# Two slabs loaded before a wait, the last recurrences split apart, late slabs four at a step, and keys prepared ahead of state loads

## The chip, the cores and the metric

The kernel runs on one core of a Trainium2 chip. The metric is the device time of one execution in microseconds (us); lower is better. The kernel before takes 1451.17 us, the median of three runs (1448.81 to 1451.53).

## The reference

One inference step of one layer of a hybrid decoder, on 512 prompt tokens and 8 sequences of 4 new tokens (544 columns in all), model width 1024, float32. Cut to what matters:

```python
h = rmsnorm(x) * (1 + sc1) + sh1                       # sh1, sc1, g1, sh2, sc2, g2 = silu(c) @ w_ada + b_ada
q, k, v, g, xr, gr = split(h @ w_in)                   # 1024,1024,2048,2048,1536,1536 wide
o, s_new = retention(rope(q), rope(k), v, s_ret)       # 4 heads, 256 x 512 states, chunks of the prompt
branch_ret = (groupnorm(o) * silu(g)) @ w_br_ret
xconv = causal_conv(xr)                                # width 4
r, i = sigmoid(xconv @ w_a + b_a), sigmoid(xconv @ w_x + b_x)     # blocks of 128
a = exp(-8 * r * softplus(-lru)); h_t = a * h_(t-1) + sqrt(1 - a*a) * (i * xconv)
branch_rnn = (h_t * gelu(gr)) @ w_br_rnn
mixed = (ga * branch_ret + gb * branch_rnn) @ w_out    # ga, gb = sigmoid(h @ w_mgate + b_mgate)
x = x + g1 * rmsnorm(mixed)
x = x + g2 * rmsnorm((silu(fg) * fu) @ w_ffn_out)      # fg, fu = (rmsnorm(x) * (1 + sc2) + sh2) @ w_ffn_in
```

The outputs are x, the new retention states, the last recurrent state and the last three inputs of the convolution.

## The kernel before

All activations stand with channels on the 128 partitions and the 544 columns in the free dimension. A weight matrix comes in **slabs** of 128 output channels: 128 x 1024 numbers (512 KB), for `w_br_rnn` two halves of 128 x 768 (384 KB) per output tile. A slab is loaded by SP into one of two `raw` buffers (`load_to`, L686), ScalarE rounds it to `w_hi` (`split_to`, L1179) and VectorE writes the rest to `w_lo` (L1510); both are rings of three. TensorE multiplies in three passes (hi*hi, hi*lo, lo*hi) with two halves of 272 columns (`three_passes`, L754), so a tile of 8 slab columns is 48 matmuls. A `raw` buffer is free when VectorE has made its `w_lo` (L693), a ring place when TensorE is through with the slab three before. ScalarE and VectorE call `ahead(key)` ahead of a tile, which splits slabs up to two behind it. Tiles alternate between two pairs of PSUM banks: a tile waits (`claim`) until the tile two before it was taken out.

The order of work is written out by hand, once per engine, and each engine runs its own list in order; SP and GpSimd also wait in order for what their DMAs need. Three stretches matter here.

**The start (0 to 75 us).** SP issues the input, 16 slabs of `w_ada` and the slabs of the first two tiles, `xr0` and `gr0` (slabs 0 and 1), and then waits until h is complete (`h_ready`, L709), since `rg_w` (the weights of the recurrent gates, 1.5 MB) and the late slabs lie where the start's buffers lay. Behind that wait it issues `rg_w`, three late slabs (`load_late(ADA_EARLY)`), and all further slabs in order. ScalarE's list behind h: split slab 2 (L1275), evacuate tile `xr0` (L1283 to L1287), split slab 3, evacuate `gr0`.

**The end of the recurrent branch (240 to 375 us).** For n = 0 to 11 the tiles are `xr n`, two gate matmuls, `gr n`, and some tiles `gb m` of the merge gate; at n = 11 four, `gb 4` to `gb 7`, with the gates of block 11 behind `gb 4`. VectorE per n: convolution, split, the recurrence of a block (`decays` and `recur`, L1609 to L1638, thirteen operations with the scan at L1634), splits. At n = 11 blocks 9, 10 and 11 are still to do. After them come eight tiles `bn m` (the projection of the recurrent branch, in two halves of six blocks each; the first tile's halves wait block by block for `y_ready`), and behind each half the modulations of two **late** slabs of `w_ada` (slabs of 512 KB; 32 in all, in a ring of 13, of which 3 places are free from the start and 10 only when the recurrences are done: `recurrences_done`, L712). SP loads late slabs and `bn` slabs in turn in the loop at L720.

**The states (400 to 950 us).** Per head, TensorE works down the tiles and small units of `retention_units` (L158). For each of 8 sequences `b` there is a unit that adds to a state (`sample`, L1040), which needs `k_st`, the keys masked to that sequence, made by GpSimd in three operations (L2060 to L2065), and pairs of sequences have cross products (`cross`, L1020), which need the state loaded. There are four state buffers. GpSimd's list per sequence (L2050): wait for the store of the state two before, load the next into its buffer, prepare the keys, and then store the state before (`store_state`, which waits for VectorE's update).

Of the kernel before, what the change touches and what calls it, by code (L numbers as in the profile page):

```python
# [31 lines left out]
KD = D // P  # L32
SEQ = 512
NB = 8
# [6 lines left out]
H = 4  # L41
# [3 lines left out]
NR = DR // P  # L45
# [27 lines left out]
STATES = 4  # L73
ADA_RING = 13
ADA_EARLY = 3
# [110 lines left out]
GATE_TILES = {1: (0,), 4: (1,), 7: (2,), 10: (3,), NR - 1: (4, 5, 6, 7)}  # L186
# [17 lines left out]
def recurrences_at(n):  # L204

    if n == NR - 1:
        return (n - 2, n - 1)
    return (n - 1,) if n == NR else (n - 2,) if n >= 2 else ()
# [156 lines left out]
def hybrid_layer_kernel(nc, w, out):  # L365
    pl = make_plan()
# [5 lines left out]
    with ExitStack() as top:  # L372
        def sem(name):
            return top.enter_context(nc.semaphore(name))
# [129 lines left out]
        s_stored = [sem(f"s_stored{i}") for i in range(STATES)]  # L504
# [97 lines left out]
        def wait_freed(eng, key):  # L602
            eng.wait_ge(*freed(key))
# [31 lines left out]
        def late_slab(n):  # L635

            i = n % ADA_RING
            return ada_late[:, i, :] if i < ADA_EARLY else ada_more[:, i - ADA_EARLY, :]
# [30 lines left out]
        @block.sync  # L669
        def _(sp):  # L670
            nxt = [0]
            late = [0]

            def load_late(n):

                while late[0] < n:
                    j = late[0]
                    if j == ADA_EARLY:
                        recurrences_done()
                    if j >= ADA_RING:  # L680
                        sp.wait_ge(late_used, j - ADA_RING + 1)
                    sp.dma_start(late_slab(j), w["w_ada"][FIRST_BLOCKS + j // KD, j % KD])\
                        .then_inc(late_in[j % ADA_RING], 16)
                    late[0] += 1

            def load_to(s):  # L686

                while nxt[0] <= s and nxt[0] < len(pl.slabs):
                    i = nxt[0]
                    key, cols = pl.slabs[i]  # L690
                    place, loaded, _, last = raw_slab(i)
                    if last is not None:
                        sp.wait_ge(lo_ready, last + 1)  # L693
                    sp.dma_start(place[:, 0:cols], slab_source(w, key)).then_inc(loaded, 16)
                    nxt[0] += 1

            def load_x(i):
                sp.dma_start(x_in[:, 2 * i:2 * i + 2, :], w["x"][:, 2 * i:2 * i + 2, :]).then_inc(x_loaded[i], 16)

            sp.dma_start(con[:], w["con"]).then_inc(con_in, 16)  # L700
            load_x(0)
            sp.dma_start(vec[:], w["vec"]).then_inc(vec_in, 16)
            for i in range(1, 4):
                load_x(i)
            for n in range(FIRST_BLOCKS * KD):
                if n == KD:
                    load_to(pl.slab[("gr", 0, "w", 0)])
                sp.dma_start(ada_raw[:, n, :], w["w_ada"][n // KD, n % KD]).then_inc(ada_in[n], 16)
            sp.wait_ge(h_ready, KD)  # L709
            sp.wait_ge(c4_ready, 1)  # L710
            sp.dma_start(rg_w[:], w["w_rg"]).then_inc(rg_in, 16)
            def recurrences_done():  # L712

                sp.wait_ge(last_saved, NR)
                sp.wait_ge(tails_saved, NR)
                sp.wait_ge(y_ready, NR)

            load_late(ADA_EARLY)
            load_to(pl.slab[("bn", 1, "w", 0)])
            for m in range(KD):  # L720
                for part in range(2):
                    load_late(min(4 * m + 2 * part + ADA_RING, 4 * KD))
                    load_to(pl.slab[("bn", m, "w", part)] + 2)
            sp.dma_start(out["rnn"], rnn_out[:]).then_inc(stored, 16)
            load_to(pl.slab[("v", 0, 1, "w", 0)])
            rnn_memory_free(sp)
            sp.dma_start(cosin[:], w["cosin"]).then_inc(cosin_in, 16)
            for h in range(H):
                load_to(pl.slab[("k", h, 0, "w", 0)])
                if h:  # L730
                    wait_freed(sp, ("sc", h - 1, JT - 1))
                sp.dma_start(dec[:], w["dec"][h]).then_inc(dec_in, 16)
            load_to(pl.slab[("wo", KD - 2 * EARLY, "w", 0)])

            sp.wait_ge(mix_ready, KD)
            states_stored(sp)
            sp.dma_start(xr_[:], w["x"]).then_inc(xres_in, 16)
            load_to(len(pl.slabs) - 1)
            for half in range(2):
                for k in range(KD):  # L740
                    sp.wait_ge(y_done, KD * half + k + 1)
                    sp.dma_start(out["y"][:, k, cols_of(half)], xr_[:, k, cols_of(half)]).then_inc(stored, 16)
            sp.wait_ge(stored, 16 * (1 + 2 * KD))
# [760 lines left out]
        def _(dve):  # L1504
# [16 lines left out]
            def ahead(key, part=0):  # L1521
                split_to(pl.slab[(*key, "w", part)] + AHEAD)
# [86 lines left out]
            def decays(n):  # L1609


                dve.wait_ge(u_ready, n + 1)
                dve.wait_ge(e_ready, n + 1)
                u, e, root = (t[:, n % 2, :] for t in (uu, ee, su))
                do(V.tensor_scalar(e, e, 1.0, None, ALU.add))
                dve.wait_ge(su_ready, n + 1)
                do(V.scalar_tensor_tensor(u, u, 1.0, e, ALU.add, ALU.mult))
                do(V.scalar_tensor_tensor(e, u, -4.0, e, ALU.add, ALU.mult))
                do(V.tensor_scalar(u, e, -0.5, -1.0, ALU.mult, ALU.add))
# [24 lines left out]
            for n in range(NR):  # L1644
                ahead(("xr", n))
                conv(n)
                ahead(("gr", n))
                for i in recurrences_at(n):
                    decays(i)
                    recur(i)  # L1650
                for m in GATE_TILES.get(n, ()):
                    ahead(("gb", m))
                    if n == NR - 1 and m == GATE_TILES[n][0]:
                        for i in recurrences_at(NR):
                            decays(i)
                            recur(i)
            for m in range(KD):
                split_to(pl.slab[("bn", m, "w", 1)] + AHEAD)
                wait_took(dve, ("gb", m))
# [307 lines left out]
        def _(pool):  # L1967
# [54 lines left out]
            def load_state(u):  # L2022
                h, b = divmod(u, NB)
                pool.dma_start(state[:, u % STATES, :, :], w["state"][b, h].rearrange("(d p) e -> p d e", p=P))\  # L2024
                    .then_inc(s_loaded[u % STATES], 16)
# [11 lines left out]
            for h in range(H):  # L2037
                for e in range(ET):
                    wait_took(pool, ("v", h, e))
                    if h and e == 0:  # L2040
                        wait_full(pool, ("tvs", h - 1))
                    do(G.tensor_copy(v3[:, e, :].rearrange("p (r c) -> p r c", r=3),
                                     vf[:, e % 2, SEQ:T].unsqueeze(1).to_broadcast([P, 3, NS])), v3_ready, wait=False)
                pool.wait_ge(k_ready, h + 1)
                if h:
                    wait_full(pool, ("tks", h - 1))
                do(G.tensor_copy(k3[:].rearrange("p d (r c) -> p d r c", r=3),
                                 k_r[:, :, SEQ:T].unsqueeze(2).to_broadcast([P, 2, 3, NS])), k3_ready, wait=False)
                wait_freed(pool, ("tks", h))
                for b in range(NB):  # L2050
                    u = h * NB + b
                    if STATES <= u + 2 < H * NB:
                        last = u + 2 - STATES
                        pool.wait_ge(s_stored[last % STATES], 16 * (last // STATES + 1))
                        load_state(u + 2)
                    if u >= 2:
                        hh, bb_ = divmod(u - 2, NB)
                        wait_full(pool, ("sn", hh, bb_, 1))

                    do(G.tensor_scalar(k_msk[:, :], k_raw[:, :], ccol("kmask", h * NB + b, 1, 3 * NS), 1.0, ALU.mult,  # L2060
                                       ALU.mult))
                    do(G.tensor_copy(k_st[:, u % 2, :], k_msk[:, :]))
                    lo = slice(2 * NS, 3 * NS)
                    do(G.tensor_tensor(k_st[lo, u % 2, :], k_msk[lo, :], k_st[lo, u % 2, :].bitcast(F32),
                                       ALU.subtract), kst_ready)  # L2065
                    if u:
                        store_state(u - 1)
            store_state(H * NB - 1)
# [108 lines left out]
```

## Time and profile before

| | |
|---|---|
| median of three runs | 1451.17 us |
| profiled execution, its own time | 1449.33 us |
| its span (first to last instruction) | 1447.5 us |
| TensorE matmul busy | 1377.7 us, 95% |
| VectorE busy | 717.9 us, 50% |
| ScalarE busy | 484.3 us, 33% |
| GpSimd busy | 181.3 us, 13% |
| granted TensorE clock, mean | 0.979 |
| DMA | 172.70 MB, mean 119 GB/s |
| slabs `raw` to landing, median | 3.4 to 3.8 us |

The profile is of one execution. Its page gives for each engine the busy share in 40 slices of the span (36 us each): TensorE reads nine tenths or more in nearly all, with lower slices at the start, at about 265, 485 and 1010 us and at the end. The same slices show the granted clock of TensorE in tenths. A wait is put down to the instruction whose semaphore came last; where an engine waits for several, the others can be nearly as late.

### The profile page before, as it was taken

What the parts mean: (1) busy time and instruction counts of PE and PEld (TensorE: products, weight loads), DVE (VectorE), ACT (ScalarE), POOL (GpSimd) and SP (SyncE); (2) the same over time, 40 slices, a digit from 0 to 9 for tenths busy, and PEclk for the clock granted to TensorE, in tenths of its full rate; (3) what the DMA queues carried; (4) which work ended last, traced back from release to release, by engine and by line L of the source; (5) the groups of instructions that cost most, each with busy time, mean ns of one, the idle gap of its engine ahead of it and who ended that gap; (6) DMA issues with size and microseconds to landing.
All of it is one profiled execution on the core that took longest, in us unless ns stands there. A gap on an engine that the chain in (4) does not pass through costs nothing.

```text
span 1447.5 us, 23984 instructions
## 1 busy us (share of the span) xinstructions
PE 1377.7 (95%) x10324; PEld 1281.7 (89%) x10324; DVE 717.9 (50%) x998; ACT 484.3 (33%) x683; POOL 181.3 (13%) x284
## 2 busy tenths in 40 slices
PE   6699999899999899999999999999799999999995
PEld 3599999788997798799889879999799999999995
DVE  4349888522242475267437624966743333332225
ACT  4277778312231231232224123336422222212221
POOL 1013222000113212212320322000000000000000
PEclk8899999999999999999999999999899999999998
DMA  8422222475424434434442443243022222222321
GB/s 340 149 70 73 74 88 74 171 283 180 159 81 147 154 103 132 163 97 141 148 166 67 138 159 133 88 162 120 0 73 88 88 88 88 88 83 81 88 87 62
DMA packets 49930, 172.70 MB, mean 119 GB/s; under 512 B 5537, under 2 KB 7713, under 8 KB 49569
## 3 DMA queue, kind: packets, MB, share of 16 engines
q1 hardware_dynamic: 39456, 135.51, 28.1%
q0 software_dynamic: 9216, 33.56, 6.6%
q10 hardware_dynamic: 1152, 2.10, 0.4%
q8 instruction: 82, 1.34, 0.4%
q14 instruction: 24, 0.19, 0.0%
HBM read 149.82 MB, written 21.32 MB: 118 GB/s over the span
## 4 chain that ended last, share of the span: by engine, by line
PE 82%; DVE 9%; ACT 3%; DMA 3%; issue 2%; POOL 0%; SPq 0%; DVEq 0%; ACTq 0%; POOLq 0%
PE ps L760 66%; PE ps L769 3%; PE ps L1005 2%; PE ps L1016 2%; PE ps L808 1%; PE ps L988 1%; PE ps L1048 1%; PE ps L1034 1%; DMA raw<-in_w_brnn 1%; PE ps L891 1%; DMA raw<-in_w_out 1%; DVE w_lo L1517 1%; DMA raw<-in_w_rnn 1%; DVE x_res L1872 1%; DVE rsn L1867 1%
## 5 line engine op out<-in xcount | busy, mean ns | idle before, releaser
L760 PE MATMUL ps<-h_hi,w_hi 128*128 128x272 f32 x2096 | 444.1, 293 | 22.8 <-ACT xs L1287 9.5
L760 PE MATMUL ps<-h_hi,w_lo 128*128 128x272 f32 x2096 | 436.3, 290 | 0.0
L760 PE MATMUL ps<-h_lo,w_hi 128*128 128x272 f32 x2096 | 435.3, 289 | 0.0
L1517 DVE TENSOR_TENSOR w_lo<-raw,w_hi 128x1024 fp32r<-128x1024 f32 (+2 forms) x190 | 226.5, 1195 | 335.3 <-ACT w_hi L1189 332.9
L760 PEld LDWEIGHTS ps<-h_hi,w_hi 128*128 128x128 f32 x2096 | 333.9, 190 | 36.6 <-issue 18.0
L760 PEld LDWEIGHTS ps<-h_lo,w_hi 128*128 128x128 f32 x2096 | 332.4, 190 | 0.0
L760 PEld LDWEIGHTS ps<-h_hi,w_lo 128*128 128x128 f32 x2096 | 330.2, 190 | 0.0
L1189 ACT ACTIVATE w_hi<-raw 128x1024 fp32r<-128x1024 f32 (+2 forms) x190 | 195.6, 1030 | 355.9 <-PE ps L760 241.5
L1791 DVE SCALAR_TENSOR_TENSOR state<-state,ps 128x512 f32<-128x512 f32 x64 | 41.1, 684 | 111.1 <-PE ps L1048 110.9
L760 PE MATMUL ps<-a_hi,w_hi 128*128 128x272 f32 x308 | 63.8, 288 | 2.1 <-DVE a_lo L1526 2.1
L760 PE MATMUL ps<-a_hi,w_lo 128*128 128x272 f32 x308 | 63.8, 288 | 0.0
L760 PE MATMUL ps<-a_lo,w_hi 128*128 128x272 f32 x308 | 63.5, 288 | 0.0
L760 PE MATMUL ps<-r_hi,w_hi 128*128 128x272 f32 x256 | 53.6, 290 | 0.0
L760 PE MATMUL ps<-r_hi,w_lo 128*128 128x272 f32 x256 | 52.9, 288 | 0.0
L760 PE MATMUL ps<-r_lo,w_hi 128*128 128x272 f32 x256 | 52.8, 288 | 0.0
L760 PEld LDWEIGHTS ps<-a_hi,w_hi 128*128 128x128 f32 x308 | 48.4, 188 | 2.3 <-DVE a_lo L1526 2.3
L760 PEld LDWEIGHTS ps<-a_lo,w_hi 128*128 128x128 f32 x308 | 48.4, 189 | 0.0
L2024 POOL DMA_DIRECT2D state<-in_state x32 | 23.4, 730 | 199.1 <-PE ps L816 104.5
L760 PEld LDWEIGHTS ps<-a_hi,w_lo 128*128 128x128 f32 x308 | 48.1, 189 | 0.0
L760 PEld LDWEIGHTS ps<-r_hi,w_hi 128*128 128x128 f32 x256 | 40.3, 188 | 5.2 <-DVE w_lo L1517 2.5
L1944 DVE TENSOR_TENSOR a_tmp<-a_tmp,ps 128x544 f32<-128x544 f32 x19 | 13.7, 721 | 60.9 <-PE ps L760 60.9
L1197 ACT ACTIVATE a_tmp<-ps 128x544 f32<-128x544 f32 x19 | 11.9, 626 | 95.2 <-PE ps L760 95.2
(238 smaller groups left out, 1848.8 us busy)
## 6 DMA issues: line engine op xcount, KB each, us to landing
raw<-in_w_head SPq DMA_DIRECT2D x48, 512.0 KB, 3.8
raw<-in_w_fin SPq DMA_DIRECT2D x38, 512.0 KB, 3.4
state<-in_state POOLq DMA_DIRECT2D x32, 512.0 KB, 4.1
out_rs<-state POOLq DMA_DIRECT2D x32, 512.0 KB, 3.9
raw<-in_w_rnn SPq DMA_DIRECT2D x24, 512.0 KB, 3.5
ada_more<-in_w_ada SPq DMA_DIRECT2D x23, 512.0 KB, 6.2
ada_raw<-in_w_ada SPq DMA_DIRECT2D x16, 512.0 KB, 14.6
raw<-in_w_bret SPq DMA_DIRECT2D x16, 512.0 KB, 3.5
```

The lines of the kernel that those rows point to most:

```text
L760: mm = nc.tensor.matmul(dst[:, half, :], a, b[:, half * HALF:(half + 1) * HALF], start=first and j == 0, stop=last and j == 2)
L769: mm = nc.tensor.matmul(dst, a, b[:, cols_of(half)], start=first and j == 0, stop=last and j == 2)
L808: mm = nc.tensor.matmul(ps[g * ROWS:(g + 1) * ROWS, bank, 0:ADA_COLS], c_rows[:, k, :], slab[:, g * ADA_COLS:(g + 1) * ADA_COLS], start=k ...
L891: mm = nc.tensor.matmul(dst[:, half, 0:HALF], rg_w[:, n, g, :], xc[:, n % 2, half * HALF:(half + 1) * HALF], start=True, stop=True)
L988: mm = nc.tensor.matmul(dst[:, 0:SEQ - j * P], k_r[:, d, j * P:(j + 1) * P], q_r[:, d, j * P:SEQ], start=d == 0, stop=d == 1)
L1005: mm = nc.tensor.matmul(dst[:, j * P:SEQ], v_tok[:, j, o * P:(o + 1) * P], scores(j), start=j == 0, stop=j == JT - 1, skip_group_check=True)
L1016: mm = nc.tensor.matmul(dst[:, :], k_tok[:, j, d * P:(d + 1) * P], v_tok[:, j, :], start=j == 0, stop=j == JT - 1)
L1034: nc.tensor.matmul(ps[g * NS:(g + 1) * NS, 7, :], q_st[:, d, NS * b:NS * (b + 1)], state[:, u % STATES, d, :], start=pair == 0, stop=pair ...
L1189: A(hi[:, 0:cols], src[:, 0:cols], ACT.Copy).then_inc(hi_ready, 1)
L1517: V.tensor_tensor(lo[:, 0:cols], raw_slab(i)[0][:, 0:cols], hi[:, 0:cols].bitcast(F32), ALU.subtract).then_inc(lo_ready, 1)
L1791: do(V.scalar_tensor_tensor(state[:, u % STATES, d, :], state[:, u % STATES, d, :], gamma(h) ** TS, ps[:, pl.bank[key][0], :], ALU.mult, A ...
L2024: pool.dma_start(state[:, u % STATES, :, :], w["state"][b, h].rearrange("(d p) e -> p d e", p=P))\
```

## The change

It has four parts, in three places.

1. `load_to(gr 1)`, which issues slabs 2 and 3, is put ahead of SP's wait for `h_ready`.
2. At n = 11 VectorE's list was: recurrences 9 and 10, splits for `gb 4`, recurrence 11, splits for `gb 5`, `gb 6`, `gb 7`. It becomes: recurrence 9, splits up to two behind `gb 4`; recurrence 10, splits up to two behind `gb 6`; recurrence 11, splits up to two behind `gb 7`.
3. In the loop of the `bn` tiles SP issues the `bn` slab first and then late slabs, at most to number 3 + 4 * (i + 1) in step i = 2m + part, where the ring's limit of 13 + 2i is not lower. Before, the late slabs came first, up to the ring's limit.
4. GpSimd prepares the keys of a sequence ahead of the wait for a store and the load of the state two further on.

```diff
--- before.py
+++ after.py
@@ -706,6 +706,7 @@
                 if n == KD:
                     load_to(pl.slab[("gr", 0, "w", 0)])
                 sp.dma_start(ada_raw[:, n, :], w["w_ada"][n // KD, n % KD]).then_inc(ada_in[n], 16)
+            load_to(pl.slab[("gr", 1, "w", 0)])
             sp.wait_ge(h_ready, KD)
             sp.wait_ge(c4_ready, 1)
             sp.dma_start(rg_w[:], w["w_rg"]).then_inc(rg_in, 16)
@@ -719,8 +720,9 @@
             load_to(pl.slab[("bn", 1, "w", 0)])
             for m in range(KD):
                 for part in range(2):
-                    load_late(min(4 * m + 2 * part + ADA_RING, 4 * KD))
                     load_to(pl.slab[("bn", m, "w", part)] + 2)
+                    i = 2 * m + part
+                    load_late(min(2 * i + ADA_RING, ADA_EARLY + 4 * (i + 1), 4 * KD))
             sp.dma_start(out["rnn"], rnn_out[:]).then_inc(stored, 16)
             load_to(pl.slab[("v", 0, 1, "w", 0)])
             rnn_memory_free(sp)
@@ -1645,15 +1647,18 @@
                 ahead(("xr", n))
                 conv(n)
                 ahead(("gr", n))
-                for i in recurrences_at(n):
-                    decays(i)
-                    recur(i)
-                for m in GATE_TILES.get(n, ()):
-                    ahead(("gb", m))
-                    if n == NR - 1 and m == GATE_TILES[n][0]:
-                        for i in recurrences_at(NR):
-                            decays(i)
-                            recur(i)
+                if n < NR - 1:
+                    for i in recurrences_at(n):
+                        decays(i)
+                        recur(i)
+                    for m in GATE_TILES.get(n, ()):
+                        ahead(("gb", m))
+                else:
+                    ends = GATE_TILES[n]
+                    for i, until in zip(recurrences_at(n) + recurrences_at(NR), (ends[0], ends[2], ends[3])):
+                        decays(i)
+                        recur(i)
+                        ahead(("gb", until))
             for m in range(KD):
                 split_to(pl.slab[("bn", m, "w", 1)] + AHEAD)
                 wait_took(dve, ("gb", m))
@@ -2049,10 +2054,6 @@
                 wait_freed(pool, ("tks", h))
                 for b in range(NB):
                     u = h * NB + b
-                    if STATES <= u + 2 < H * NB:
-                        last = u + 2 - STATES
-                        pool.wait_ge(s_stored[last % STATES], 16 * (last // STATES + 1))
-                        load_state(u + 2)
                     if u >= 2:
                         hh, bb_ = divmod(u - 2, NB)
                         wait_full(pool, ("sn", hh, bb_, 1))
@@ -2063,6 +2064,10 @@
                     lo = slice(2 * NS, 3 * NS)
                     do(G.tensor_tensor(k_st[lo, u % 2, :], k_msk[lo, :], k_st[lo, u % 2, :].bitcast(F32),
                                        ALU.subtract), kst_ready)
+                    if STATES <= u + 2 < H * NB:
+                        last = u + 2 - STATES
+                        pool.wait_ge(s_stored[last % STATES], 16 * (last // STATES + 1))
+                        load_state(u + 2)
                     if u:
                         store_state(u - 1)
             store_state(H * NB - 1)
```

## Rows read from the trace of the kernel before

**Rows 1.** Waits of TensorE by what they waited for: us in total, times, longest.

```profile
PE ps L760 <- ACT xs L1287: 9.5, 1, 9.5
...
PE ps L760 <- DVE w_lo L1517: 8.5, 4, 5.9
...
PE ps L1048 <- POOL k_st L2064: 4.8, 1, 4.8
```

**Rows 2.** The chain that ended last in order of time: start, us, what.

```profile
52.53 9.54 DMA raw<-in_w_rnn
...
64.68 7.84 PE ps L760 x48
...
309.75 4.73 PE ps L760 x36
...
438.19 6.02 PE ps L760 x48
...
485.73 7.11 PE ps L760 x48
```

**Rows 3.** Windows of 5 us: busy us (instructions) of each engine, clock, DMA, GB/s.

```profile
35.00:40.00 5.00, 5.00 (x48) 3.62 (x48) 0.09 (x1) 0.00 (x0) 0.00 (x0) 1.00 0.00 0
...
60.00:65.00 5.00, 0.32 (x1) 0.35 (x2) 1.65 (x2) 2.85 (x6) 0.33 (x1) 0.50 0.48 196
...
285.00:290.00 5.00, 5.00 (x48) 4.66 (x50) 0.00 (x0) 0.00 (x0) 0.00 (x0) 1.00 1.03 410
```

**Rows 4.** Timeline of 28 to 110 us: start, us, engine, line, operation, idle before.

```profile
33.86 1.23 DVE L1517 TENSOR_TENSOR w_lo<-raw,w_hi 128x1024 fp32r<-128x1024 f32 x1
...
50.60 0.33 SPq L711 DMA_DIRECT2D rg_w<-in_w_rg  x1
...
54.81 0.41 PE L760 MATMUL ps<-h_hi,w_lo 128*128 128x272 f32 x2
...
62.15 1.06 ACT L1189 ACTIVATE w_hi<-raw 128x1024 fp32r<-128x1024 f32 x1 [12.40 <-DMA raw<-in_w_rnn]
```

**Rows 5.** Timeline of VectorE, 242 to 312 us.

```profile
252.97 0.73 DVE L1526 TENSOR_TENSOR y_lo<-bb,y_hi 128x544 fp32r<-128x544 f32 x1
...
253.73 0.45 DVE L1615 TENSOR_SCALAR ee<-ee 128x544 f32<-128x544 f32 x1
...
260.84 1.74 DVE L1526 TENSOR_TENSOR y_lo<-bb,y_hi 128x544 fp32r<-128x544 f32 x1
...
262.61 1.23 DVE L1517 TENSOR_TENSOR w_lo<-raw,w_hi 128x1024 fp32r<-128x1024 f32 x1
```

**Rows 6.** Timeline of TensorE, 242 to 306 us.

```profile
263.98 0.79 PE L760 MATMUL ps<-h_hi,w_hi 128*128 128x272 f32 x2 [5.92 <-DVE w_lo L1517]
...
279.08 0.42 PE L760 MATMUL ps<-y_hi,w_hi 128*128 128x272 f32 x2
...
298.28 0.52 PE L760 MATMUL ps<-y_hi,w_hi 128*128 128x272 f32 x2 [2.11 <-DVE w_lo L1517]
```

**Rows 7.** Timeline of ScalarE, 242 to 312 us.

```profile
246.45 1.05 ACT L1189 ACTIVATE w_hi<-raw 128x1024 fp32r<-128x1024 f32 x1
...
257.77 1.04 ACT L1189 ACTIVATE w_hi<-raw 128x1024 fp32r<-128x1024 f32 x1
```

**Rows 8.** Timeline of GpSimd, 242 to 312 us.

```profile
260.46 1.52 POOL L1995 TENSOR_TENSOR ii<-ii,xc 128x544 f32<-128x544 f32 x1
```

**Rows 9.** Timeline of SP's queue, 242 to 312 us.

```profile
274.17 6.03 SPq L682 DMA_DIRECT2D ada_more<-in_w_ada  x10
...
285.22 0.43 SPq L694 DMA_DIRECT2D raw<-in_w_brnn  x1
```

**Rows 10.** Timeline of TensorE, 476 to 494 us.

```profile
484.51 1.22 PE L1048 MATMUL ps<-v_st,k_st 96*128 96x512 f32 x2 [4.75 <-POOL k_st L2064]
```

**Rows 11.** Timeline of GpSimd, 395 to 560 us.

```profile
478.15 0.78 POOL L2031 DMA_DIRECT2D out_rs<-state  x1 [0.32 <-POOL k_st L2064]
...
482.43 0.77 POOL L2060 TENSOR_SCALAR k_msk<-k_raw,con 96x256 f32<-96x256 f32 x1
```

## The prediction

> **What bounds the kernel now.** The page first: TensorE is busy 95% of the span and heads the chain that ended last, so what can be won is what it waits for. The view of waits says what that is: one wait of 9.5 us on ScalarE's evacuation, four of 8.5 us in all on VectorE's weight splits, one of 4.8 us on GpSimd's masked keys [rows 1]. The three code regions of the diff lie at these three places. The timeline around each then shows why the wait is there, and the chain what a tile costs at either clock: 48 matmuls take 6.02 us, and 7.84 and 7.11 us behind two of these waits [rows 2] (the windows show the granted clock at 0.50 of full speed in 60 to 65 us, which is 1.2 GHz [rows 3]). So each wait costs more than its length.
>
> **Part A, two slabs before the wait for h.** Slab 2 (the second input tile, xr1) and slab 3 (gr1) are issued only at 52.53 us, behind the recurrent weights (1.5 MB) and three late slabs (0.5 MB each), and the first lands 9.54 us later [rows 2, 4]. ScalarE stands at its split until 62.15, and only then evacuates tile 0, for whose bank TensorE waits: its last matmul begins at 54.81, the next tile at 64.68 [rows 2, 4]. `load_to(gr1)` itself waits for the VectorE splits of slabs 0 and 1; the second begins at 33.86 and ends at 35.1 [rows 4]. So both loads are issued by 35.2 us, and the queue is empty in 35 to 40 us (0 GB/s) [rows 3]; they land about 4 us later, long before h is complete at 50.6. SP waited for h anyway, so nothing is queued behind the new wait. Then ScalarE splits slab 2 (1.06), VectorE follows (1.23): about 53.1, earlier than TensorE's end at 55.22; ScalarE evacuates tile 0 by about 53.7. What was next on the queue: the recurrent weights, issued at 50.60, are first in a backlog that was all through by 62.07 with two slabs more in it [rows 2, 4], and are wanted after xr1, at about 61.2 (1.5 MB is 3.8 us at the 410 GB/s of [rows 3]). Slab 4 (gb0) will be issued at 53.1 and land at 61 to 62; it is wanted at 55.2 + 6.0 + 1.8 + 6.0 = 69. ScalarE is held by it for some 2 us after xr1's end and has gr1's 6 us to make this up. Gain: 9.46 of wait and 7.84 - 6.02 = 1.82 of slow clock, 11.3 us. Bounds: 0, if ScalarE found another load late, and 11.3. I take 11.3, for every wait on the way has a row with room.
>
> **Part B, the last recurrences and the late slabs.** Before, VectorE runs two recurrences between two splits: recurrence 10 begins at 253.73, and the split that tile gb6 needs comes at 262.61 [rows 5]. Tile gb5 ends at 263.98 - 5.92 = 258.06, gb6 starts at 263.98, bn0 at 279.08 [rows 6]: 21.02 us for two tiles that take 12.04, so 8.98 lost. After the change the split stands at 253.73 (its ScalarE half is done: 246.45 [rows 7]), ends at 254.96, and gb6 starts at 258.06 without a wait, to 264.1. Recurrence 10 takes 262.61 - 253.73 = 8.88 us, to 263.8, and the split of gb7 behind it (ScalarE half 257.77 [rows 7]) ends at 265.0: a new wait of about 1.0 us. Of the 8.88 one microsecond is a collision: the same subtraction takes 0.73 us once and 1.74 where GpSimd multiplies beside it [rows 5, 8]. The product in question waits for the same scan and moves with it, so I keep the collision; without it the wait is 0.
> The Trainium skill, SBUF — State Buffer, section "SBUF: two separate sides", calls this an exclusive lock: GpSimd and a VectorE operation with two SBUF inputs take turns for a whole instruction. The trace agrees with 1.74 against 0.73 us, and by that rule the collision stays; were it chance, part B would give 1.0 us more.
> Recurrence 11 then begins after the splits of gb7 and bn0's first half (0.96), at 266.0 instead of 263.75, and ends by 273.9 (7.9 us without a collision), with bn0's second split at 274.8. TensorE: gb7 265.1 to 271.1, bn0's first half 4.73 us and the two modulations 1.00 [rows 2], so it wants the second half at 276.8. That covers it by 2 us; it holds because the first half needs recurrences 0 to 5 only.
> The queue: before, ten late slabs from 274.17 and two more stand ahead of bn slab 3, issued at 285.22, and TensorE waits 2.11 us for it at 298.28 [rows 6, 9], the queue being full at 410 GB/s [rows 3]. After, the order on SP is four late, bn slab 3, four late, bn slab 4, four late, bn slab 5, from 273.9 on. At 0.41 MB per us (late 0.52, bn 0.39 MB): slab 3 is through at 280, slab 4 at 286, slab 5 at 292; 2.3 us more for both splits. They are wanted at 288.3, 294.0 and 299.7 (steps of 5.73 us). Room 5 us. Late slabs are taken two at a step and come four at a step: number 3 is wanted at 281.5 and is there by 276. From the fourth step both orders load to the same number and SP waits for the same use, with the bn load now ahead. So 2.11 goes. Part B: 8.98 - 1.0 + 2.11 = 10.1 us. Bounds: 4 (the 2.5 us that a slow clock took from the tile at 263.98, 8.5 instead of 6.0, come back, slab 3's 2.11 stay, and another step waits 1.5) and 11.1.
>
> **Part C, keys ahead of loads.** TensorE stands 4.75 us before 484.51 for the keys of sample 7 [rows 10]. On GpSimd the store of state 5 (478.15, 0.78) comes first, then a wait for the store of state 5 to land and a load (to 482.34), then three operations, from 482.43 to TensorE's start at 484.51, 2.08 us [rows 10, 11]. After: the store no later than 478.15, the keys at once, from 479.0 to 481.1 (478.15 + 0.78 + 2.08 and 0.1 between). TensorE is free at 484.51 - 4.75 = 479.76: a wait of 1.35 is left. With the tile after it at full speed (7.11 - 6.02 = 1.09 [rows 2]) the gain is 4.75 - 1.35 + 1.09 = 4.5 us. The moved loads are late by those three operations at most, 2 us, and in every step the store they wait for takes as long or longer. The view of waits has no row in which TensorE waits for a state's load. The other 31 preparations stand behind nothing that TensorE waits for: 0. Bounds: 2.4 (the collision above on one more operation, +1, and the slow clock kept) and 5.8.
>
> **Sum.** 11.3 + 10.1 + 4.5 = 25.9. The profiled execution took 1449.33 us (span 1447.5), so 1423.4. It lies 1.8 us under the median of the three runs, 1451.17, from which it would be 1425.3; I say 1424. Nothing behind the three places is late next: the page's slices of TensorE are nines between them, VectorE and ScalarE are below that, and both shift with it.
>
> **Rivals.**
> 1. The small new waits (1.0 and 1.35 us) keep a slow stretch behind them: 2.5 + 1.1 us back, 1427.5. For it: a wait of 4.75 us was enough [rows 2, 10]. Against: the 2.11 us at 298.28 was followed by pairs at full speed. Chance 0.10.
> 2. Part A moves the wait: ScalarE takes slab 4's split before it evacuates xr1, so with a late slab 4 (backlog in front of it) TensorE stands before gb0. For a full return slab 4 would have to land 7 us later than worked out: 1435. Chance 0.06.
> 3. Part B's VectorE chain slips: recurrence 11 ends after 276.8, with more collisions, and every bn step waits about a microsecond for its slab: 1430. Against: 2 us of cover. Chance 0.08.
> 4. Slower: the late slabs. SP waits for a bn split before it issues the next four late slabs; if a late slab came after TensorE wanted it, each of the last 13 steps would hold a whole landing, 13 x 3.5 = 45 us, and the time would be 1468. It decides where late slab 2i lands after step i begins. Against: at the second step the lead is 5 us, and it grows by two slabs a step. Chance 0.02.
> The forecast itself 0.74.
>
> **Numbers.** Range 1419 to 1431: below, the waits of 1.0 and 1.35 vanish and the run-to-run spread of 2 us; above, rivals 1 and 3, with rival 2 left out. About 0.2% (3 us) is what can be told from no change. Faster 0.95, same 0.02, slower 0.03.
>
> **What would show it.** Right: xr1's tile starts within 0.5 us of the tile before it, the granted clock is 1.00 in the windows there; gb6 follows gb5 at once; TensorE's waits on w_lo are below 2 us in all; the wait on k_st is 1 to 2 us. Wrong: ScalarE waiting for in_w_gb while TensorE stands, a wait on late slabs at the modulations, a wait on a y tile in bn0, or clock windows under 1.00 behind the small waits.

## The result and the profile after

The kernel after takes 1430.2 us, the median of four runs (1426.68 to 1431.54), against 1451.35 us (1448.81 to 1451.81): a ratio of 0.9854 (95% interval 0.9832 to 0.9876). That is 21 us less. The forecast was 1424, 27 us less (its terms add up to 25.9), and 1430.2 lies inside the range, near its upper end. Timed again in two later sets, the same kernel took 1424.88 (1423.18 to 1428.01) and 1424.80 us (1422.10 to 1426.03), 0.9823 and 0.9816 of the kernel before, so 25.5 and 26.4 us less. It varies more from run to run than the forecast allowed, and the experiments below find the larger part of that in part C.

The page of the profiled execution (1431.27 us in all):

```profile
span 1429.5 us, 24013 instructions
...
PE 1376.7 (96%) x10324; PEld 1281.1 (90%) x10324; DVE 718.4 (50%) x998; ACT 483.9 (34%) x683; POOL 178.4 (12%) x284
...
PE   6899999999998999999999999998899999999995
```

TensorE does the same work in 18.0 us less. The lower slice at about 265 us is gone; an 8 is left in the slice of 429 to 464 us, where the keys of sample 7 are prepared. Its waits (us in total, times, longest) tell why. The row on ScalarE's `xs` [rows 1] is gone, 8.5 us on `w_lo` became 1.3, and 4.8 on `k_st` only 3.8:

```profile
PE ps L1050 <- POOL k_st L2065: 3.8, 1, 3.8
...
PE ps L762 <- DVE a_lo L1528: 2.5, 1, 2.5
...
PE ps L762 <- DVE w_lo L1519: 1.3, 2, 1.1
```

The chain that ended last (start, us, what), at the places that [rows 2] shows and at the last long stretch of matmuls, which begins at 1298.19 in the kernel before and takes 116.02 us there:

```profile
48.24 14.83 PE ps L762 x96
...
64.91 18.05 PE ps L762 x144
...
452.01 6.68 DMA out_rs<-state
...
465.16 8.37 PE ps L762 x48
...
1278.61 117.56 PE ps L762 x924
```

How far the kernel after is ahead of the one before can be read off at these places, as a difference of starts. The tile behind xr1 and its gate matmuls starts at 64.91 against 74.35: 9.44 us from part A. At the end of the `bn` tiles the lead is 19.63 (354.72 against 374.35), so part B gave 10.2. Behind the tile at 465.16 it is 19.31, although the wait there is shorter: that tile took 8.37 us against 7.11 [rows 2]. The rest up to 1278.61 adds 0.27, and the last stretch takes 1.54 longer: 18.04 in all.

**Part A in the trace.** SP's queue in the first 60 us (start, us, instruction). Slabs 2 and 3 are issued from 26.93 on, ahead of the wait for h:

```profile
26.93 8.39 SPq L694 DMA_DIRECT2D raw<-in_w_rnn  x2
51.71 0.33 SPq L712 DMA_DIRECT2D rg_w<-in_w_rg  x1
...
54.13 0.33 SPq L694 DMA_DIRECT2D raw<-in_w_gb  x1
```

ScalarE from 40 us on: it splits slab 2 as soon as h is done and evacuates tile xr0 at 54.09. Its long wait is now for slab 4 and ends at 63.21, when TensorE has just left xr1 (63.07) for its gate matmuls, which find their bank free:

```profile
51.72 1.06 ACT L1191 ACTIVATE w_hi<-raw 128x1024 fp32r<-128x1024 f32 x1 [0.86 <-DVE h_lo L1538]
54.09 0.81 ACT L1285 ACTIVATE xc<-ps,vec 128x544 f32<-128x544 f32 x1 [1.31 <-PE ps L762]
...
63.21 1.06 ACT L1191 ACTIVATE w_hi<-raw 128x1024 fp32r<-128x1024 f32 x1 [4.80 <-DMA raw<-in_w_gb]
```

**Part B.** VectorE around the last recurrences. The split for gb6 stands at 244.28 and costs no wait. The collision predicted for the subtraction behind recurrence 10 is there, 1.77 us at 252.52, and the split of gb7 comes behind it:

```profile
244.28 1.23 DVE L1519 TENSOR_TENSOR w_lo<-raw,w_hi 128x1024 fp32r<-128x1024 f32 x1
...
252.52 1.77 DVE L1528 TENSOR_TENSOR y_lo<-bb,y_hi 128x544 fp32r<-128x544 f32 x1
254.32 2.09 DVE L1519 TENSOR_TENSOR w_lo<-raw,w_hi 128x1024 fp32r<-128x1024 f32 x2
...
264.20 1.83 DVE L1519 TENSOR_TENSOR w_lo<-raw,w_hi 128x768 fp32r<-128x768 f32 x2
```

GpSimd's product beside it is the operation of [rows 8], and SP's queue holds the order late, `bn`, late, `bn`:

```profile
252.15 1.56 POOL L2000 TENSOR_TENSOR ii<-ii,xc 128x544 f32<-128x544 f32 x1
```

```profile
264.25 1.75 SPq L682 DMA_DIRECT2D ada_more<-in_w_ada  x4
266.05 0.76 SPq L694 DMA_DIRECT2D raw<-in_w_brnn  x1
266.85 2.10 SPq L682 DMA_DIRECT2D ada_more<-in_w_ada  x4
269.01 0.51 SPq L694 DMA_DIRECT2D raw<-in_w_brnn  x1
```

**Part C.** GpSimd in head 0. The store of state 4 is issued at 452.01, the keys of sample 6 follow, and then GpSimd stands 4.32 us until that store has landed. Only behind it come the load of state 8, the store of state 5, and the keys of sample 7, two of whose three operations are longer than at 453.70 (0.40, 0.73):

```profile
449.78 0.77 POOL L2029 DMA_DIRECT2D state<-in_state  x1 [3.19 <-DMA out_rs<-state]
452.01 0.73 POOL L2036 DMA_DIRECT2D out_rs<-state  x1 [1.46 <-DVE state L1796]
...
459.24 0.77 POOL L2029 DMA_DIRECT2D state<-in_state  x1 [4.32 <-DMA out_rs<-state]
460.01 0.73 POOL L2036 DMA_DIRECT2D out_rs<-state  x1
...
461.37 1.36 POOL L2063 CAST k_st<-k_msk 96x256 fp32r<-96x256 f32 x1
462.81 1.08 POOL L2065 TENSOR_TENSOR k_st<-k_msk,k_st 32x256 fp32r<-32x256 f32 x1
```

The waits of TensorE that parts B and C leave:

```profile
255.69 0.49 PE L762 MATMUL ps<-h_hi,w_hi 128*128 128x272 f32 x2 [1.08 <-DVE w_lo L1519]
...
463.94 1.22 PE L1050 MATMUL ps<-v_st,k_st 96*128 96x512 f32 x2 [3.81 <-POOL k_st L2065]
```

### The profile page after: what moved, and what is told of

The parts are those of the page before. It is cut to its first block, busy times and chain, and to the rows that moved or that the text cites. A ratio compares the mean times of both kernels' runs of the same rounds, so it can differ in the third digit from the quotient of the medians.

```text
span 1429.5 us, 24013 instructions
## 1 busy us (share of the span) xinstructions
PE 1376.7 (96%) x10324; PEld 1281.1 (90%) x10324; DVE 718.4 (50%) x998; ACT 483.9 (34%) x683; POOL 178.4 (12%) x284
## 4 chain that ended last, share of the span: by engine, by line
PE 83%; DVE 9%; ACT 3%; issue 2%; DMA 2%; POOL 0%; SPq 0%; DVEq 0%; ACTq 0%; POOLq 0%
PE ps L762 69%; PE ps L1007 2%; PE ps L771 2%; PE ps L1018 2%; PE ps L810 1%; PE ps L990 1%; PE ps L1050 1%; PE ps L1036 1%; DVE rsn L1872 1%; DVE x_res L1877 1%; PE ps L893 1%; DMA raw<-in_w_out 1%; DVE mo L1876 1%; DVE w_lo L1519 1%; ACT w_hi L1191 1%
```

## The experiments

There were three sets of four kernels; each set has its own runs of the kernel before (medians 1450.42, 1450.37, 1451.23 us), and a gain is the difference from that. 0.1% is 1.4 us.

### Each part alone

**Part A alone**: the kernel before with one line more.

```diff
+            load_to(pl.slab[("gr", 1, "w", 0)])
             sp.wait_ge(h_ready, KD)
```

> The kernel before with the one moved load of slabs 2 and 3 alone. Theory (the whole wait was the slab's landing): the wait of 9.5 us on ScalarE's evacuation is gone, TensorE starts xr1's tile at once behind gr0; with the slow stretch behind the wait gone too 11.3 us faster, 1440 against 1451; in the trace between 9 and 12 us, by how long the slow stretch of the start lasts in that run. The other waits (w_lo 8 us, k_st 4.8 us) stay. Rival (ScalarE found another load late): gain under 5 us and a new wait before gb0.

Measured: 1439.08 us (1438.27 to 1441.29), ratio 0.9919 (0.9906 to 0.9932), a gain of 11.3 us, which is the term of the sum. The profiled run is the slowest of the five (1441.29), and at the tile behind xr1's gate matmuls it is 9.44 us ahead, as the kernel after is.

**The splits of part B alone**: the rewrite of VectorE's list at n = 11, SP's loop as before.

```diff
+                    for i, until in zip(recurrences_at(n) + recurrences_at(NR), (ends[0], ends[2], ends[3])):
+                        decays(i)
+                        recur(i)
+                        ahead(("gb", until))
```

> The kernel before with the splits between the last recurrences alone. Theory: gb6 follows gb5 at once, gb7 waits 1.1 us, bn0 starts 7.9 us earlier against the end of gb5; the wait on bn slab 3 stays at about 2 us or grows, since TensorE comes to it 8 us earlier while ten late slabs still stand ahead of it in the queue, all held until recurrence 11 is done. That recurrence ends later against gb5's end by 2 us, and the slab lands later by as much: the wait grows to 2 + 8 + 2 = 12 us if the queue alone decides. Then the net gain is near 0 (1451), and the two halves of part B belong together. Rival (slabs land with TensorE's pace): gain 8 us, 1443.

Measured: 1449.90 us (1448.97 to 1452.54), ratio 1.0000 (0.9992 to 1.0009): nothing. TensorE's waits in its timeline (in brackets: us and what ended them):

```profile
264.77 0.49 PE L760 MATMUL ps<-h_hi,w_hi 128*128 128x272 f32 x2 [1.05 <-DVE w_lo L1517]
...
295.17 0.82 PE L760 MATMUL ps<-y_hi,w_hi 128*128 128x272 f32 x2 [7.21 <-DVE w_lo L1517]
```

The 5.92 us before gb6 [rows 6] became 1.05 before gb7, and the wait for `bn` slab 3 grew from 2.11 to 7.21. TensorE arrives there 8.2 us earlier (287.96 against 296.17). The slab, in the old order behind the late ones on a full queue, lands only 3.1 us earlier (293.3 against 296.4). The longer wait takes 5.1 of the 8.2 us, and a slow stretch behind it takes 2.1 more. The granted clock is 0.51 in 295 to 300 us, and the half tile takes 6.87 us instead of 4.74:

```profile
295.17 6.87 PE ps L760 x36
```

The expectation had the wait at 12 us if the queue alone decides; it was 7.2, and the net was near nothing, as expected.

**The late slabs alone**: SP's loop as after, VectorE's list as before.

```diff
-                    load_late(min(4 * m + 2 * part + ADA_RING, 4 * KD))
                     load_to(pl.slab[("bn", m, "w", part)] + 2)
+                    i = 2 * m + part
+                    load_late(min(2 * i + ADA_RING, ADA_EARLY + 4 * (i + 1), 4 * KD))
```

> The kernel before with the new order of late slabs alone. Theory: the wait of 2.1 us on bn slab 3 is gone and nothing else moves, 2 us faster (1449); late slabs are never waited for. Rival: late slabs come too late for their modulation and TensorE waits at L808's line.

Measured: 1449.62 us (1448.74 to 1451.01), ratio 0.9994 (0.9986 to 1.0003), 0.8 us. The waits of 5.94 us before gb6 and 0.25 before gb7 are left; the one for `bn` slab 3 is gone. Its 2.1 us show in their place: at the end of the `bn` tiles this profile is 2.3 us ahead of the one before (372.03 against 374.35). It loses 1.0 in the tile behind the wait for `k_st` (8.14 us against 7.11) and 1.5 in the last long stretch of matmuls (117.55 against 116.02), none of which the edit touches.

**Part C alone**: GpSimd's new order in the kernel before.

```diff
                     u = h * NB + b
-                    if STATES <= u + 2 < H * NB:
-                        last = u + 2 - STATES
-                        pool.wait_ge(s_stored[last % STATES], 16 * (last // STATES + 1))
-                        load_state(u + 2)
...
                                        ALU.subtract), kst_ready)
+                    if STATES <= u + 2 < H * NB:
+                        last = u + 2 - STATES
+                        pool.wait_ge(s_stored[last % STATES], 16 * (last // STATES + 1))
+                        load_state(u + 2)
```

> The kernel before with the keys ahead of the loads alone. The blind reading expected 4.5 us less. After the result: the keys of sample 7 still stand behind the load of state 8, and loads and stores are now issued 0.8 us apart, so that a store lands after 5 to 7 us instead of 3.3. Theory now: the wait on k_st is 3.5 to 4.5 us instead of 4.75 and the slow stretch behind it stays; 0 to 1.5 us faster (1450). Rival (the other parts disturbed part C in the changed kernel, for example through the phase of SP's loads): the wait falls to 1.4 us and the time by 3 to 4.5 us.

Measured: 1443.33 us (1442.55 to 1448.18), ratio 0.9956 (0.9944 to 0.9968), a gain of 7.1 us (4.6 to 8.1 by the interval). GpSimd's timeline and the chain:

```profile
470.69 0.73 POOL L2031 DMA_DIRECT2D out_rs<-state  x1 [1.90 <-DVE state L1791]
...
475.74 0.77 POOL L2024 DMA_DIRECT2D state<-in_state  x1 [2.16 <-DMA out_rs<-state]
477.18 0.73 POOL L2031 DMA_DIRECT2D out_rs<-state  x1 [0.67 <-DVE state L1791]
478.00 0.47 POOL L2056 TENSOR_SCALAR k_msk<-k_raw,con 96x256 f32<-96x256 f32 x1
```

```profile
480.51 6.02 PE ps L760 x48
```

Here the step goes as forecast, and not as in the expectation (3.5 to 4.5 us of wait, 0 to 1.5 gained): its rival had the wait right and the gain too small. The load that waits for the store of state 4 is issued 5.05 us behind it, in time. The keys start at 478.00; this profile is 0.97 us ahead of the one before (470.69 against 471.66), so that is 479.0 in its time, as forecast. TensorE waits 0.97 us, and the tile behind runs at full speed.

### Parts together

**Part B whole, in the kernel before** (both edits above).

> The kernel before with both halves of part B, splits and late order, without A and C. Each alone was worth 0.5 and 0.8 us. Theory (each removes the wait that takes the other's place: with the splits alone the wait for bn slab 3 grew from 2.1 to 7.2 us): together 9 to 10 us, 1441. Rival (they add up): 1.3 us, 1449.

Measured: 1441.27 us (1439.89 to 1441.87), ratio 0.9933 (0.9920 to 0.9945), 10.0 us where the two halves give 0.5 and 0.8. Its one wait above a microsecond between 242 and 306 us is 1.08 before gb7.

**A and B, without C**: the kernel after with the refill (the wait and the load) ahead of the keys again.

> The changed kernel without part C (loads ahead of keys, as before). Theory: the wait of 4.8 us on k_st and its slow stretch are back whole, 1451 - 11.3 - 10.1 = 1429 to 1430: little more than the changed kernel where its part C fails, 4 to 7 us more than where it works. Rival: without C the time stays that of the changed kernel to within 0.5 us in the median, then C is worth nothing beside A and B.

Measured: 1430.36 us (1428.56 to 1430.87), ratio 0.9859 (0.9845 to 0.9872), 20.0 us. Parts A and B add up as forecast, to 21.3 alone and 20.0 together.

**The kernel after, twice more.**

> The changed kernel once more. With part C alone the keys of sample 7 came in time (wait about 1 us, no slow stretch, 7 us faster) when the store of state 4 landed after 4.5 us, and in the changed kernel's profile they came late (wait 3.8 us, slow stretch) when it landed after 6.7 us. Theory: part C in the changed kernel stands at the edge of this landing and runs fall on both sides: times from about 1425 to 1431. In the profile the wait on k_st goes with the landing of that store: above about 5.5 us a wait of 2 to 4 us, below 1 us. Rival (the other parts always disturb C): all runs near 1430, wait 3.8 us.

> The changed kernel a third time, for the spread of its part C: the profile's wait on k_st was 3.8 us (1431.3) and 1.8 us (1428.0) so far. Theory: again between 1 and 4 us, times between 1423 and 1432, and always above last-keys-first in the median. Rival: the first set was another chip's, and this is 1424 to 1425 as the second.

Measured: 1424.88 and 1424.80 us, above. So part C beside A and B is worth 5.5 us by the set that has both; by the first runs of the kernel after it would be 0.2. The profiles furthest apart (spans 1429.5 and 1423.3) differ by 5.5 us between the store of state 4 and the end of the tile behind sample 7. What differs there is one race. GpSimd's own rows in each profile (us; landing is the issue of the store of state 4 to that of the load of state 8, which waits for it):

| kernel | load of 7 ahead of the store by | landing | wait for `k_st` | tile behind it |
|---|---|---|---|---|
| before | 3.69 | 3.64 | 4.8 (store of 5) | 7.11 |
| A and B | 3.82 | 3.68 | 4.7 (store of 5) | 7.52 |
| C alone | 2.67 | 5.05 | 1.0 | 6.02 |
| after, third | 2.47 | 5.89 | 1.1 | 6.02 |
| after, again | 2.29 | 6.52 | 1.8 | 7.54 |
| one slab (below) | 2.21 | 6.94 | 3.1 | 7.36 |
| after | 2.23 | 7.23 | 3.8 | 8.37 |

In the order of after a load is issued closer ahead of the store, and the store lands later; the load that waits for it holds back the keys of sample 7. A slab of SP is in flight too, but it is issued 1.3 us behind this store in all seven profiles, so it is not what differs between them. Why the time from load to store varies within one kernel is open. The expectation's rival, that the first set ran on another chip, is not excluded either: the second and the third set ran on two different chips and have the same median, and the chip of the first is not on record. The last section adds the stores without a slab beside them.

### What the mechanism allows

**The store ahead of the refill.**

```diff
+                    if u:
+                        store_state(u - 1)
                     if STATES <= u + 2 < H * NB:
...
-                    if u:
-                        store_state(u - 1)
```

> The changed kernel with the store of a state ahead of the load behind the keys (order: keys, store, load). Theory (load and store issued 0.8 us apart share the queue, and the one in front lands in 3.3 us): stores land in 3.2 to 4 us again, most of all that of state 4; but the load of state 8 now waits behind the store of state 5 and still stands ahead of the keys of sample 7, so these are ready 1.3 to 2.3 us after TensorE wants them in every run: about 1425 to 1427 with little spread. Rival (SP's slabs and ScalarE's stores make the landings long): stores of state 2 to 4 still take 5 to 7 us.

Measured: 1456.46 us (1453.41 to 1459.20), ratio 1.0043 (1.0030 to 1.0057): slower than before. The expectation was wrong by 30 us. The new row in TensorE's waits:

```profile
PE ps L1036 <- DMA state<-in_state: 19.4, 8, 3.1
```

The wait for `k_st` is gone, but each load now stands behind a store that waits for VectorE's update of the state. The loads come late, a row that none of the other kernels has. It is 19.4 of the 31.6 us over the kernel after of its set; the rest was not followed. How long a store takes to land can't be read here, since no load had to wait for one.

**The last keys of a head ahead of both refills.** Samples 6 and 7 prepare their keys first; then refill, two stores, refill.

```diff
-                    if STATES <= u + 2 < H * NB:
...
+                    if b == NB - 2:
+                        continue
+                    if b == NB - 1:
+                        refill(u - 1)
+                        store_state(u - 2)
+                        store_state(u - 1)
+                        refill(u)
+                        continue
+                    refill(u)
                     if u:
                         store_state(u - 1)
```

> The changed kernel, where samples 6 and 7 of each head have their keys prepared ahead of all DMAs of these two steps (the load and store of step 6 move behind the keys of sample 7; the loads are of the next head's states). Theory: TensorE does not wait on k_st at all in head 0, no slow stretch follows, whatever the landings: 1 us of wait less than part C at its best, 6 us less than the changed kernel's profile: 1424 to 1425, and little spread. Rival 1: a new wait on the load of a state at the next head's cross products, or on a state's store at the end. Rival 2 (the gain is C's at its best only): 1425 to 1426.

Measured: 1422.15 us (1421.72 to 1424.15), ratio 0.9807 (0.9793 to 0.9820), 28.2 us under the kernel before, 8.2 under A and B, and 2 less than expected. GpSimd's timeline: the keys wait for TensorE's read of sample 5's, and the refill comes behind them.

```profile
455.47 0.47 POOL L2067 TENSOR_SCALAR k_msk<-k_raw,con 96x256 f32<-96x256 f32 x1 [2.10 <-PE ps L1050]
...
456.48 0.72 POOL L2071 TENSOR_TENSOR k_st<-k_msk,k_st 32x256 fp32r<-32x256 f32 x1
457.50 0.77 POOL L2029 DMA_DIRECT2D state<-in_state  x1 [0.30 <-POOL k_st L2071]
```

The chain at the same places, first of this kernel, then of A and B:

```profile
459.56 6.02 PE ps L762 x48
...
1271.38 115.78 PE ps L762 x924
```

```profile
463.85 7.52 PE ps L762 x48
...
1277.41 116.02 PE ps L762 x924
```

The tile behind sample 7 starts without a wait and at full speed. The two spans (1420.5, 1426.8) are 6.3 us apart: 4.7 of wait, 1.5 of the tile and 0.3 of the pair of matmuls between them, less 0.7 by which this profile was behind when xr1 was done; the last stretch and what lies before it add 0.2 each. This is the fastest kernel of the study.

**The same, with the split of gb7 inside recurrence 10**, behind its scan:

```diff
+                if between is not None:
+                    ahead(between)
                 wait_took(dve, ("gr", n))
```

> The last-keys-first kernel, and the split of gb7's slab moved into recurrence 10, behind its scan. Theory: the wait of 1.1 us before gb7 is gone, recurrence 11 and bn0 keep their distance, 1.1 us faster than last-keys-first: 1421. Rival: the split there collides with GpSimd's product and pushes it and recurrence 11 back, so that bn0's second half waits: no gain or a loss of 1 us.

Measured: 1422.59 us (1422.10 to 1423.09), ratio 0.9807 (0.9793 to 0.9820): no gain that can be measured over the kernel without it. TensorE's waits on `w_lo` are 0.2 us instead of 1.3, so the edit does in its place what was expected. From the start of the tile behind xr1's gate matmuls to the last long stretch this profile gains 2.0 us on the one without the split (it goes from 0.6 behind to 1.4 ahead, 1269.94 against 1271.38), and that stretch then takes 1.8 us more (115.78 without the split):

```profile
1269.94 117.56 PE ps L762 x924
```

The collision moved to the conversion (0.44 us elsewhere), here on VectorE and beside it GpSimd's product:

```profile
252.19 1.63 DVE L1527 CAST y_hi<-bb 128x544 fp32r<-128x544 f32 x1
```

```profile
252.17 1.35 POOL L2002 TENSOR_TENSOR ii<-ii,xc 128x544 f32<-128x544 f32 x1
```

**One slab ahead of h instead of two.**

```diff
-            load_to(pl.slab[("gr", 1, "w", 0)])
+            load_to(pl.slab[("xr", 1, "w", 0)])
             sp.wait_ge(h_ready, KD)
```

> The changed kernel with only slab 2 (xr1) issued ahead of the wait for h; slab 3 (gr1) stays behind rg_w and the late slabs. Theory: slab 2 carries the gain, TensorE starts xr1 at once; slab 3 lands at about 62, ScalarE splits it before it takes gr0's tile out, so TensorE comes to gr1 at 63 to 65 and waits 1 to 3 us for bank or split: 1 to 3 us slower than the changed kernel (1425 to 1430 in its own runs). Rival: slab 3 in time, no difference; or both needed, 9 us back.

Measured: 1428.79 us (1427.33 to 1430.12), ratio 0.9849 (0.9836 to 0.9863), 4.0 us over the kernel after of its set. TensorE's timeline shows the wait one tile later, behind a slab that lands 9.77 us after its issue at 52.72:

```profile
65.55 0.52 PE L762 MATMUL ps<-h_hi,w_hi 128*128 128x272 f32 x2 [2.24 <-ACT gelu L1298]
```

The second slab is worth that wait of 2.24. The rest of the 4.0 is not shown. This profile also has a longer wait for `k_st` (3.1 against 1.1) and a longer tile behind it (7.36 against 6.02), which the kernel after shows in some runs too; whether the single slab makes that more frequent, one profile can't tell.

## Why the prediction was right, and where not

**Part A, 11.3 forecast, 11.3 measured alone.** Where TensorE waited and why, and slab 4's late landing that only ScalarE feels: all as worked out. The profiles of part A alone and of the kernel after show 9.44 only. In the latter h was complete at 51.71 instead of 50.60 us, which is 1.1, and the 96 matmuls from 48.24 took 14.83 us where the forecast allows 14.1, behind a longer stretch at the lower clock (14.1 to 14.8 in the eight profiles with both slabs ahead). The forecast had no term for either. That this is chance is not shown: h was complete at 50.25 to 52.12 us in those eight profiles and at 50.24 to 50.98 in the six with one slab or none ahead.

**Part B, 10.1 forecast, 10.2 in the profile, 10.0 alone.** The waits of 1.08 (forecast 1.0) and none at 298.28 are the two that it named, the collision among them. By the Trainium skill (SBUF — State Buffer, section "SBUF: two separate sides") GpSimd and a VectorE operation with two SBUF inputs take turns for a whole instruction; the trace agrees, with 1.77 us against 0.73 for the subtraction. With the split moved in front, the conversion paid instead (1.63 against 0.44). What the forecast did not say is that the splits need the late order: without it their gain goes into the wait for `bn` slab 3 and the slow stretch behind it. Written as a sum, 8.98 - 1.0 and 2.11 look like separate gains of 8.0 and 2.1; alone they are 0.5 and 0.8. The 2.1 of the late order did come in its place, as its profile shows, and was lost again behind it; the 8.0 of the splits did not.

**Part C, 4.5 forecast, about zero in the first profile (5.5 us beside A and B in the second set, 7.1 alone): the step that failed.** It reads "After: the store no later than 478.15, the keys at once, from 479.0 to 481.1", and "The moved loads are late by those three operations at most, 2 us, and in every step the store they wait for takes as long or longer." The refill of the sample before stands ahead of this store and these keys. It waits for the store of state 4, for whose landing the forecast kept, without saying so, the time of the old order, 3.64 us. In the new order the landing takes 5.05 to 7.23, and a late landing is a wait of TensorE: 1.1 us at 5.89, 3.8 at 7.23. Of these 2.7 more, 1.3 are the landing itself and 1.3 the two key operations that are stretched in that profile (1.36 and 1.08 us against 0.40 and 0.73). Where the landing was short the forecast holds to 0.4 us of wait (part C alone); in that profile the 6.4 us between the spans (1447.5, 1441.1) are 3.8 of wait, 1.09 of clock, 0.49 for the pair of matmuls right behind the wait (1.22 [rows 10], then 0.73), which the forecast left out, and the 0.97 by which it was already ahead, most of it from a shorter wait for `bn` slab 3. Putting the last keys ahead of that refill and of the store of state 5 removes the wait.

**Rival 1**, a slow stretch behind small new waits, is true for part C where the wait was longer than forecast. Behind the waits of 1.0 and 1.1 us at either place the tile ran at full speed in every profile. Behind 1.8 to 3.8 us it took 7.36 to 8.37. It named the clock alone, 1427.5; what brings the first runs to 1430.2 is the longer wait as much as the clock. **Rival 2** (slab 4 late) did not occur; its mechanism is what one slab alone shows. **Rival 3** did not occur: bn0's second split starts at 264.20 and takes 0.96, so it ends 2.3 us before TensorE wants it at 267.45 (forecast 2). **Rival 4** did not occur in these orders: no wait on a late slab grew.

The 7.9 us between the forecast for the profiled execution (1423.4) and its time (1431.27) are thus 1.9 in part A and 1.5 in the last stretch, for neither of which it had a term, and 4.8 in part C, less 0.4 elsewhere. In the profile of the third set the same marks give 10.5, 10.2 and 5.2 us for parts A, B and C, less 1.9 behind them (1.5 of it in the last stretch), 24 in all. So the medians of 1424.9 and 1424.8 are close to the 1424 in part by luck: a last stretch that nobody forecast, against a part C that gave more than its 4.5.

## What to carry to other kernels

Before two waits are added up, ask whether the later one is set by a queue that does not move with the engine: then removing the first mostly lengthens the second, and both edits have to be made at once. When a DMA is moved in an in-order list, look one step back in that list at every wait that now stands ahead of the urgent work, and give the landing it waits for a range, since the move changes what is in flight beside it. Put the small urgent work ahead of all such waits, but do not put a load behind a store that waits for compute.

## What the runs showed of the hardware

**The same wait, with and without a slow stretch.** TensorE waits 2.5 us for `a_lo` at the last long stretch in the kernel after, in A and B and in the fastest one, and the 924 matmuls behind it took 117.56, 116.02 and 115.78 us. In windows of 5 us (busy us of TensorE, weight loads, VectorE, ScalarE and GpSimd, then the granted clock, DMA share and GB/s) the clock of the kernel after is lower there:

```profile
1277.00:1282.00 5.00, 3.39 (x17) 3.39 (x18) 2.58 (x4) 0.18 (x1) 0.00 (x0) 0.73 0.26 69
1282.00:1287.00 5.00, 5.00 (x39) 5.00 (x39) 0.00 (x0) 0.48 (x1) 0.00 (x0) 0.93 0.06 24
```

This did not vary from run to run of one kernel: the three profiles of the kernel after show 117.56, 117.56 and 117.54. It changed with edits far ahead of it, 117.56 with the split inside recurrence 10 and 115.78 without; what decides is open. An edit worth 1.5 us can be hidden by it or doubled.

At the start it does vary between runs. The 96 matmuls behind the wait for h took 14.83, 14.80 and 14.32 us in the three profiles of the kernel after. The Trainium skill (TensorE: Matmul & The Clock Gate, section "What's actually happening") says that how many matmuls run at the lower clock at a kernel's start varies from run to run; the trace agrees as far as these three go.

The length of a slow stretch does not follow the wait either. Behind the same wait of 4.75 us for `k_st` the tile took 7.10 to 8.14 us in six profiles, and behind 1.8 us it took 7.54.

**Landing of a store.** The 512 KB of state 4 landed in 3.6 to 3.7 us with a load issued 3.7 to 3.8 us ahead on GpSimd's queue, and in 5.0 to 7.2 us with one 2.2 to 2.7 us ahead, a slab of SP beside it each time. The store of state 3 has no slab beside it, since the last one was issued over 8 us earlier (it takes 5.0 us to land in the first kernel, 5.9 in the second). From its issue to that of the load behind it, first in the kernel before, then in after:

```profile
464.55 0.78 POOL L2031 DMA_DIRECT2D out_rs<-state  x1 [0.30 <-POOL k_st L2064]
467.97 0.72 POOL L2024 DMA_DIRECT2D state<-in_state  x1 [2.64 <-DMA out_rs<-state]
```

```profile
444.04 0.73 POOL L2036 DMA_DIRECT2D out_rs<-state  x1
```

That is 3.42 us with a load 2.84 us ahead, and 5.74 (to 449.78) with one 0.77 ahead; six more profiles with this order for sample 5 have 5.7 to 5.9. So in these profiles a load close ahead goes with a late store without any slab. With the load far ahead the slab hardly matters (3.64 against 3.42); with it near, the two together gave the longest landings. GpSimd's waiting list turned that directly into waiting of TensorE.
